# Strassen's seven products in the down-projection of three of the five FFN tiles of a hybrid decoder layer

## The reference, cut to what matters

```python
h = rmsnorm(x, g_pre_ffn)
upc, new_ffn = causal_dwconv(h @ w_up, buf_ffn, w_ffn_conv)       # (B,T,2*D_FF), D_FF = 2816
gate, val = jnp.split(upc, 2, axis=-1)
y = (jax.nn.silu(gate) * val) @ w_down                            # 2816 -> 1024
x = x + rmsnorm(y, g_post_ffn)
```

## Time and profile before

| | |
|---|---|
| time, median of 3 runs | 806.68 us (806.6 to 807.78) |
| span of the profiled execution, slowest core (2) | 812.6 us |
| spans of cores 4 to 7 in it | 803.4 to 803.8 us |
| TensorE busy on core 2 | 798.6 us of 812.6 (98%) |
| VectorE, ScalarE, GpSimd busy | 551.9, 447.8, 255.3 us |
| chain that ended last | TensorE 92% of the span |

### The profile page before, as it was taken

The page is one execution under the profiler, slowest core; times in us unless marked ns, Lnnn a source line. Parts: engine busy times, 40 slices in busy tenths (PEclk is TensorE's granted clock), DMA queues, the critical chain, the costliest instruction groups (busy, mean ns, idle before and its releaser), DMA issues.

```text
span 812.6 us, 15177 instructions; the slowest of 8 cores (803.4 to 812.6 us)
## 1 busy us (share of the span) xinstructions
PE 798.6 (98%) x4500; PEld 438.4 (54%) x4500; DVE 551.9 (68%) x990; ACT 447.8 (55%) x1012; POOL 255.3 (31%) x268
## 2 busy tenths in 40 slices
PE   7999999999999999999999999999999999999997
PEld 5444455555555555554545555555555555576764
DVE  3897448896986785677989553766557655576566
ACT  3433284675565644586676444745447444576553
POOL 5542002001201144489534322342223422233124
PEclk9999999999999999999999999999999999999999
DMA  9999805856215989998972874472223722249736
GB/s 181 200 164 155 158 4 116 186 141 133 70 41 122 188 140 196 160 157 122 180 184 47 131 146 131 102 137 79 72 72 71 133 95 72 73 84 228 269 109 219
DMA packets 76543, 107.00 MB, mean 132 GB/s; under 512 B 12432, under 2 KB 65808, under 8 KB 76448
## 3 DMA queue, kind: packets, MB, share of 16 engines
q0 software_dynamic: 38992, 43.11, 37.9%
q1 hardware_dynamic: 37472, 62.94, 25.6%
HBM read 107.34 MB, written 29.03 MB: 168 GB/s over the span
## 4 chain that ended last, share of the span: by engine, by line
PE 92%; DMA 3%; DVE 2%; issue 2%; ACT 1%; DVEq 0%; ACTq 0%; POOLq 0%; POOL 0%
PE ps L510 92%; DMA big<-xT 2%; DMA big<-w_in 1%; DVE big L597 0%; DVE big L765 0%; DVE big L767 0%; DVE big L761 0%; ACT L568 0%; DVEq L1200 0%; DVE big L654 0%; ACT big L1079 0%; ACT big L568 0%; DVE big L660 0%; ACT big L748 0%; DVE big L706 0%
## 5 line engine op out<-in xcount | busy, mean ns | idle before, releaser
L510 PE MATMUL ps<-big 128*128 128x392 bf16 (+7 forms) x4482 | 798.0, 341 | 8.8 <-ACT big L1058 2.0
L510 PEld LDWEIGHTS ps<-big 128*128 128x128 bf16 x4482 | 435.0, 98 | 367.2 <-issue 16.2
L883 DVE SCALAR_TENSOR_TENSOR big<-ps,big 128x456 f32<-128x456 f32 (+2 forms) x440 | 253.4, 636 | 125.2 <-ACT big L876 108.8
L897 POOL TENSOR_TENSOR big<-big 128x448 bf16<-128x448 f32 (+2 forms) x110 | 119.0, 1084 | 263.4 <-ACT big L896 185.2
L879 ACT ACTIVATE big<-ps,big 128x448 f32<-128x448 f32 (+2 forms) x220 | 126.7, 598 | 18.6 <-PE ps L510 11.5
L896 ACT ACTIVATE big<-big 128x448 f32<-128x448 f32 (+2 forms) x110 | 59.9, 545 | 45.9 <-DVE big L883 44.0
L748 ACT ACTIVATE big<-ps 128x392 f32<-128x392 f32 (+1 forms) x80 | 39.2, 514 | 57.7 <-PE ps L510 29.1
L873 ACT ACTIVATE ps<-big 128x4 f32<-128x4 f32 (+1 forms) x100 | 17.6, 176 | 94.5 <-PE ps L510 94.1
L521 POOL DMA_DIRECT2D big<-xT x16 | 14.9, 958 | 164.5 <-DVE big L808 104.3
L523 POOL DMA_DIRECT2D big<-w_up x44 | 32.5, 756 | 54.3 <-PE ps L510 49.4
L761 DVE SCALAR_TENSOR_TENSOR big<-ps,big 128x392 f32<-128x392 f32 (+1 forms) x40 | 25.8, 645 | 31.5 <-PE ps L510 31.4
(11 more groups left out here) (74 smaller groups left out, 394.7 us busy)
## 6 DMA issues: line engine op xcount, KB each, us to landing
big<-w_dnb SPq DMA_DIRECT2D x32, 704.0 KB, 5.0
big<-w_up POOLq DMA_DIRECT2D x44, 256.0 KB, 14.8
big<-w_in POOLq DMA_DIRECT2D x32, 256.0 KB, 22.1
big<-xT POOLq DMA_DIRECT2D x16, 392.0 KB, 7.8
big<-w_dn POOLq DMA_DIRECT2D x8, 704.0 KB, 10.8
w_dnb<-big SPq DMA_DIRECT2D x8, 704.0 KB, 5.7
big<-xT SPq DMA_DIRECT2D x6, 784.0 KB, 6.0
yT<-big SPq DMA_DIRECT2D x6, 784.0 KB, 7.1
```

The lines of the kernel that those rows point to most:

```text
L510: ins = e.matmul(o, lhsT=l, rhs=x, start=(start and i == 0), stop=(stop and i == last))
L883: dve(lambda e, b=b, fj=fj, tt=tt, k=k: e.scalar_tensor_tensor(out=tt[:, 0:n], in0=ps[:, b * 512 + k:b * 512 + k + n], scalar=cc(C_WF + 44 ...
L897: S.add("pool", lambda e: e.tensor_tensor(out=gb.ap[:, j, 0:N], in0=g, in1=v, op=ALU.mult), [T.t()], [gb.t(j, 1)], dur=N * 2.17 + 100)
```

## The change

Tiles 2, 3 and 4 of the FFN (`t` 1 to 3) get their down-projection by Strassen's method. The weights (2816 by 1024) are split in four quarters, rows halves of 11 hidden blocks each and output halves of 4 blocks each; a tile's hidden values are split by the same 11 and 11 blocks and by left and right half of its columns. Seven products A to G of quarter size replace eight. Each product is done in two steps (`md`) of 22 matmuls of half the tile's width, 11 into the left and 11 into the right part of a bank, so a tile has 14 steps.

- The tile widths become 448, 464, 448, 448 and 256. The pairs run in the order 0, 11, 1, 12 and so on (`JORD`), with the columns of `w_up` re-ordered by the host as before.
- The sums of weight quarters (5 kinds) are made once, by VectorE in `wsum`, out of the ring's slots while the first tile's down-projection uses them: 4 calls, two placed at pairs 17 and 20 of tile 1, two after steps 1 and 3 of tile 1's down-projection, which is in tile 2. Each result goes through a small staging buffer (`WST`) to memory (`w_dns`) on SyncE's queue. The first two calls make 5 sums of 1408 elements each, the last two 10 of 768 or 640.
- The sums of hidden values (`sumb`, 5 per tile, over 11 blocks by half the columns, bf16) are on VectorE; of tile 4 (`t == 3`) sums C, D and E are on GpSimd in pieces of 4 blocks.
- A step's result goes to `Y` by ScalarE (`put`) where it is the first, and is added by VectorE (`acc`) where it is not: per tile 8 `put` and 16 `acc`. The squares are taken from `Y` at the end (4 of twice the width).
- The ring has three slots for these tiles, filled by one load of 704 KB per step. Products C and D of tile 4 and the last tile's weights read the buffers `WQ`, filled piece by piece in tile 5. `X3`, `G4B` and `XTOK` are loaded inside tile 5 as well.
- Three sets of `TB` in all tiles (before: five from tile 3 on).
- `epi_y` works with 8 instructions that also apply the norm's weight, and is issued inside the same tile as the steps.
- In tile 5 the sample columns are left out of the pairs and done for all blocks at once after the last pair (`sample_cols`).

Python of the change, cut to its core:

```diff
-TB_N = (448, 456, 448, 456, 256)
+TB_N = (448, 464, 448, 448, 256)
+JORD = [j for i in range(FH) for j in (i, FH + i)]
...
+    def wsum(m):
+        bufs = [W_DN[(2 * m + i) % NW] for i in range(2)]
+        for v, ((r0, h0), (r1, h1), op) in VSUM.items():
+            for c, (lo, n) in enumerate(((0, HW),) if m < 2 else ((0, 768), (768, HW - 768))):
+                o = WST[m // 2][st_rr[0] % len(WST[m // 2])]
...
+                dve(lambda e, o=o, i0=i0, i1=i1, op=op, n=n: e.tensor_tensor(out=o.flat[:, 0:n], in0=i0, in1=i1, op=op),
+                    [x.t() for x in (bufs[r0], bufs[r1])], [o.t()], n, rate=2.0)
+                sp_dma(w_dns[v, m, :, lo:lo + n], o.flat[:, 0:n], [o.t()], [("wds", v, m, c)], 128 * n * 2)
...
+    def sw_load(s):
+        if s >= len(RING):
+            return
+        _, p, md = RING[s]
+        buf = W_DN[s % NR]
+        src, dep = w_src(p, md)
+        sp_dma(buf.flat.rearrange("p (m c) -> p m c", m=2), src, dep, [buf.t()], 128 * 2 * HW * 2, after=[last_pe[0]])
...
-        T = TB[set_rr[0] % (3 if t < 2 else 5)]
+        T = TB[set_rr[0] % 3]
...
+    def wdown(t, i):
+        p, md = STEPS[i]
...
+        for mi in range(2):
+            pe([(bank(b, mi * h + h, mi * h), wb[:, mi, k, :], rhs[:, k, :]) for k in range(FH)], [wk] + rt, [("ps", b)], h,
+               start=True, stop=True)
+        if s is not None:
+            sw_load(s + NR)
...
+        if p == "A":
+            put(4, 1)
+            put(0, 0)
+        elif p == "B":
+            acc(0, 0, ALU.add)
+        elif p == "C":
+            put(4, 0)
+            acc(0, 0, ALU.add)
+        elif p == "D":
+            put(0, 1, -1.0)
+            acc(4, 1, ALU.subtract)
+        elif p == "E":
+            acc(4, 1, ALU.subtract)
+        elif p == "F":
+            acc(4, 0, ALU.add)
+            acc(4, 1, ALU.subtract)
+        else:
+            acc(0, 0, ALU.subtract)
+            acc(0, 1, ALU.add)
...
-    WD = {5: 0, 7: 1, 10: 2, 12: 3, 14: 4, 16: 5, 19: 6, 21: 7}
-    WD1 = {9: 0, 11: 1, 13: 2, 15: 3, 17: 4, 19: 5, 20: 6, 21: 7}
-    WDL = {3: 0, 5: 1, 7: 2, 10: 3, 12: 4, 14: 5, 16: 6, 19: 7}
+    WD = [(6, 7, 9, 11, 13, 15, 17, 19), range(4, 18), (4, 5, 6, 7, 8, 9, 10, 10, 11, 12, 12, 13, 14, 14), range(4, 18)]
+    EPY = (20, 19, 16)
...
+            if t == 0 and j in (17, 20):
+                wsum(j // 20)
...
+                    if i in (1, 3):
+                        wsum(2 + i // 2)
...
+                    if i == 0:
+                        sumb(t - 1, "A")
+                    wdown(t - 1, i)
+                    if i in (0, 1, 2, 4):
+                        sumb(t - 1, {0: "B", 1: "C", 2: "D", 4: "E"}[i])
```

269 lines of the change are left out of this document (187 added, 82 removed).

## The result

The changed kernel takes 810.15 us in the median of 20 runs (806.8 to 814.12), the kernel before on the same chip 807.18 (20 runs). The ratio is 1.0036, 95% interval 1.0024 to 1.0049: slower by about 0.4%, where 800.5 us and 0.8% faster were forecast. The two kernels and all experiments are compared by undisturbed executions; where I call a kernel "without a ratio", nearly every execution had some cores at a mean clock of about 0.958.

A forecast was written before the change was run, and what follows sets the result against it. TensorE was taken to bound all of the FFN. The terms -11.5 + 0.7 + 1.3 + 2.0 + 1.3 = -6.2 us gave a median of 800.5 us, 0.8% faster, range 796 to 807.

The forecast's parts named there:

- TensorE's gain: Down-projections of three FFN tiles: 29,920 fewer matmul columns, less the cost of 396 more matmuls, gain 11.5 us.
- Rival 3: Weight loads not hidden under 224-column matmuls: 11.3 us lost, 811.8 us; chance 0.03.
- None is full, so in the mean this work is free: VectorE's added work in tiles 2 to 5 costs nothing in the mean, at 78 of 101 us in tile 2.
- Rival 2: VectorE becomes the bound of tiles 3 and 4: 3 to 5 us in the middle, about 804.5 us; chance 0.14.
- (c): Start of tile 5: short pairs let VectorE hardly regain ground; about 2 us lost (0 to 4).
- 1.45 for 2552: VectorE's price for a bf16 sum of 2552 elements (11 x 232): 1.45 us.
- (a): Seam of tiles 1 and 2: weight sums put VectorE further behind; 0.7 us lost (0 to 3).
- (b): Weight sums in tile 2: VectorE blocked by DMAs; 1.3 us lost (0 to 8).
- Rival 1: Weight sums block VectorE on DMAs for longer in tile 2, tile 3's ring loads late: 810 us, slower; chance 0.13.
- (d): End of tile 5: seven pairs without a step between, ScalarE full; 1.3 us lost (0 to 3).
- The rest ... I count nothing: GpSimd's sums and the ring's loads counted as nothing, upper bound one late load, 2 us; ScalarE a little less work.
- A change of core 4's span is a change of the median: The 2.9 us between core 4's span and the median stay unchanged; core 4 goes to 797.6 us.

The follow-up runs named there:

- v1: u3 with the eight epi_y multiplications in a row only for FFN tile 3's result; 804.23 us, of the executions compared 803.2, ratio 0.9937.
- u1: Changed kernel with each of VectorE's sums of 11 blocks issued as one of 6 and one of 5; 807.51 us, ratio 0.9995.
- u3: Changed kernel with halved sums, all eight epi_y multiplications in a row and the first weight sums held back; 804.08 us, ratio 0.9955.
- e2: Changed kernel without the four accumulating DMAs that add FFN tile 3's result to the output; 805.94 us, ratio 0.9978.
- s2: Changed kernel with the eight g4 multiplications of epi_y in a row (priority -30000 instead of -4000); 809.78 us, ratio 1.0028.
- e1: Changed kernel with the weight sums' VectorE work left out, unsummed quarters written by the same DMAs; 840.6 us, without a ratio.
- e4: Changed kernel without the weight sums' VectorE work and without the accumulating DMAs of FFN tiles 1 to 3; 833.12 us, without a ratio.
- s1: Changed kernel with tile 1's four w_dn loads issued after pairs 8, 10, 12, 14 instead of 12, 14, 16, 18; 843.7 us, without a ratio.
- s3: Changed kernel with both edits of s1 and s2; 839.62 us, without a ratio.
- t1: Changed kernel with the first ten weight sums made after pairs 1 and 6 of tile 2; 813.62 us, ratio 1.0065.
- t3: t1 with the first four of the eight epi_y multiplications in a row too; 829.37 us, of the executions compared 819.55, ratio 1.0137.
- t4: t3 with VectorE's sums of 11 blocks halved; 835.8 us, of the executions compared 810.1, ratio 1.0036.

## Why the prediction was wrong, step by step

**TensorE's gain was right.** Tile 3 took "about 97 us" in the forecast and takes 97.30 in v1, without a gap: 352 x 448 + 308 x 232 = 229,152 columns are 95.5 us, and 660 x 2.5 ns 1.65. From start to start 224 columns are 95.8 ns apart in the changed kernel, 232 columns 99.15, 256 columns 109.2. By these the gain is 11.5 us, as forecast. Rival 3 is out. The prediction also read the load time of the Trainium skill (106.7 ns for 128 columns; page TensorE: Matmul & The Clock Gate, section LDWEIGHTS (loading the stationary operand)) as a floor under every matmul. The trace does not agree with that reading, 95.8 ns apart with a new weight block each, and the measurement decides.

**"None is full, so in the mean this work is free"** is the step that failed, together with "what can cost is a stretch ... I see four". VectorE's work in tiles 2 and 3 was forecast within 1 us. But at 80% busy a single instruction of 3.5 us, or eight of 0.6 in a row, is late enough at the right place to empty the banks; u1 shows it (1.2 us at 530 and at 630, gone when a sum is two). Rival 2 named this, at 3 to 5 us; it is 2.5. (Its worst case is also added up wrong: 42 x 0.2 and 2 more for (c) are 10.4, where the prediction has 8.) The price of a sum, "1.45 for 2552", holds for 539.88 but not beside GpSimd's work. The trace before had such pairs, and I did not bound them. On its core 4 the sums of 1568 elements take 0.96 us where they stand alone, and here:

```profile
207.22 1.84 POOL L1023 TENSOR_TENSOR big<-big 128x704 f32<-128x704 f32 x1
207.42 2.47 DVE L556 TENSOR_TENSOR big<-big 128x1568 bf16<-128x1568 bf16 x1
```

**(a) The seam** was charged 0.7 us (0 to 3) by counting VectorE's work; it lost 1.5 to 4.7, and up to 1.5 more to the clock. The wait for `w_dn` was looked for in tile 2, (b), and not in tile 1, where the DMA share is 1.04 in the very rows I read the earlier trace rows. I took a load's landing from the median of the earlier trace rows, 10.5 us, where in this stretch it is 14. The eight cores side by side and u3 settle it.

**(b)** was charged 1.3 and cost nothing: TensorE has no gap from 428 to 500 us on any core. Rival 1 was right in kind, and even its 810 us is met, but at another place and price.

**(c) and (d)** were right: 2.6 for 2.0, and 1.15 for 1.3. Part of (c), 1.5 us, goes with the accumulating DMAs of tile 3 (e2), so it is not due to short pairs alone.

**"The rest ... I count nothing"** missed ScalarE's `put` behind the accumulating DMA: 0 to 3.2 us, different on each core.

**"A change of core 4's span is a change of the median"** failed for the same reason. Core 4 was forecast at 797.6; the median core is 803.2, 5.6 us more. The slowest of eight is another 5.3 us later, and 1.7 us lie around it, together 7.0, where I had put 2.9: 4.1 us more. 5.6 + 4.1 = 9.7 us is the miss of 9.65. More than half of it is mean stalls, the rest the spread of the cores. The spread is only in part that of the waits: in the profiled executions of the changed kernel and of v1, 3.0 and 4.0 us of it are there before FFN tile 1, in the token mixer. What makes it was not looked into.

## What to carry to other kernels

An engine with 20% to spare is not free: look at what stands in its queue with a foreign wait in front of it, above all a DMA in a stretch where the DMA share is near or over 1; issuing such a load earlier gave back 4 of 11 us at the landing on one core and nothing on another, moving its reader behind the real landing did away with the wait. Put long instructions in pieces where others must get between them. With all cores running the same program, price the slowest: a wait that ends with a DMA is different on each (0 to 3.2 us for the same one here), and the time follows the worst. First take off what the cores differ by before the changed part begins.

## What the hardware showed that I had not expected

After 3.33 us of idle time at the seam the granted clock was 0.62 in the mean of the next 3.3 us, worth 1.5 us; after 1.15 us of idle time it was not lowered. The length of the idle time alone does not decide it: on core 3 of the changed kernel the clock was 0.51 from 416.6 to 420 us after 2.37 us idle, on core 4 of s2 it stayed at 1.00 after 3.23 us.

A VectorE sum and a GpSimd product that both read SBUF took turns: the one that began first kept its time (1.48 us for the sum, 1.14 for the product), and the second ended 1.34 us (the sum) or 1.0 us (the product) after the first, about its own time alone.

In the kernels with stalls of 4.3 us or more on most cores (e1, e4, s1, s3, t1, t3, t4) 32 of 52 executions had both cores of a pair at a mean clock between 0.952 and 0.963, and of the 195 executions of all other kernels none had. Core 2 of s1 lost no time to waits from 400 to 600 us, and yet:

```profile
440.00:500.00 60.00, 60.00 (x258) 27.84 (x257) 38.52 (x61) 24.14 (x62) 15.74 (x14) 0.81 0.79 166
...
600.00:700.00 100.00, 98.83 (x682) 65.67 (x681) 78.10 (x121) 54.05 (x133) 31.16 (x26) 1.00 0.53 134
```

0.81 is between the two levels. Cores 0 and 1 of the same die kept 0.99 over the span. It cost cores 2 and 3 about 20 us. What sets it off was not tried; that the long stalls do is only suggested by which kernels have it.
